# Attention of a two-layer diffusion trunk: the probabilities of wide head pairs are divided by their sums before they are turned

## The reference, cut to what matters

```
def one_block(q_blk):
    s = jnp.einsum('bqkgd,btkd->bkgqt', q_blk, k, preferred_element_type=jnp.float32) * scale
    p = jax.nn.softmax(s, axis=-1).astype(v.dtype)
    return jnp.einsum('bkgqt,btkd->bqkgd', p, v)
```

## Time and profile before

| | us |
|---|---|
| time, median of 3 runs | 3545.4 (3539.25, 3545.4, 3545.46) |
| the profiled execution: its time | 3544.38 |
| the profiled execution: its span, first to last instruction | 3542.6 |
| TensorE matmuls busy | 3365.2 (95% of the span) |
| VectorE busy | 1865.5 (53%) |
| ScalarE busy | 1164.7 (33%) |
| GpSimd busy | 421.8 (12%) |
| mean granted clock of TensorE | 0.983 of full speed |

### The profile page before, as it was taken

The page is one execution under the profiler, slowest core; times in us unless marked ns, Lnnn a source line. Parts: engine busy times, 40 slices in busy tenths (PEclk is TensorE's granted clock), DMA queues, the critical chain, the costliest instruction groups (busy, mean ns, idle before and its releaser), DMA issues. The chain is left out here.

```text
span 3542.6 us, 69052 instructions
## 1 busy us (share of the span) xinstructions
PE 3365.2 (95%) x28748; PEld 2885.1 (81%) x28748; DVE 1865.5 (53%) x2801; ACT 1164.7 (33%) x1778; POOL 421.8 (12%) x286
## 2 busy tenths in 40 slices
PE   6999999999888899999999999999999978889999
PEld 5888888885668878888888888888885668779897
DVE  4552554665765555543544552554644755555353
ACT  3321222226652233322222331222226533244231
POOL 2000002004313211000001000002004333120000
PEclk9999999999999999999999999999999999999999
DMA  5222221440000012222221221221430000022222
GB/s 196 98 95 67 94 92 61 144 155 30 2 17 3 3 54 78 94 96 67 100 86 58 100 100 65 96 92 53 147 112 30 2 18 3 15 83 91 93 89 95
DMA packets 68262, 263.49 MB, mean 74 GB/s; under 512 B 7536, under 2 KB 8688, under 8 KB 67440
## 3 DMA queue, kind: packets, MB, share of 16 engines
q1 hardware_dynamic: 67648, 256.95, 21.2%
q10 hardware_dynamic: 432, 3.88, 0.3%
HBM read 258.70 MB, written 2.10 MB: 74 GB/s over the span
## 5 line engine op out<-in xcount | busy, mean ns | idle before, releaser
L240 PE MATMUL ps<-hn_hi,w_hi 128*128 128x512 f32 (+1 forms) x3520 | 872.4, 329 | 16.1 <-DVE hn_lo L447 5.9
L240 PE MATMUL ps<-hn_hi,w_lo 128*128 128x512 f32 (+1 forms) x3520 | 873.4, 329 | 0.0
L240 PE MATMUL ps<-hn_lo,w_hi 128*128 128x512 f32 (+1 forms) x3520 | 868.8, 328 | 0.0
L217 ACT ACTIVATE w_hi<-raw 128x1024 fp32r<-128x1024 f32 (+1 forms) x300 | 338.6, 1129 | 1380.3 <-PE ps L240 1222.7
L222 DVE TENSOR_TENSOR w_lo<-raw,w_hi 128x1024 fp32r<-128x1024 f32 (+1 forms) x300 | 396.7, 1322 | 481.5 <-ACT w_hi L217 473.6
L240 PEld LDWEIGHTS ps<-hn_hi,w_hi 128*128 128x128 f32 x3520 | 547.5, 190 | 83.4 <-issue 17.7
L240 PEld LDWEIGHTS ps<-hn_lo,w_hi 128*128 128x128 f32 x3520 | 547.9, 190 | 61.3
L240 PEld LDWEIGHTS ps<-hn_hi,w_lo 128*128 128x128 f32 x3520 | 544.2, 190 | 61.1
L240 PE MATMUL ps<-g_hi,w_hi 128*128 128x512 f32 (+1 forms) x1424 | 398.3, 347 | 6.8 <-DVE g_lo L881 6.8
L240 PE MATMUL ps<-g_lo,w_hi 128*128 128x512 f32 (+1 forms) x1424 | 404.0, 351 | 0.0
L240 PE MATMUL ps<-g_hi,w_lo 128*128 128x512 f32 (+1 forms) x1424 | 398.6, 347 | 0.0
(11 more groups left out here) (272 smaller groups left out, 4241.2 us busy)
## 6 DMA issues: line engine op xcount, KB each, us to landing
raw<-wgu SPq DMA_DIRECT2D x176, 512.0 KB, 3.6
w_mod_one<-wmod SPq DMA_DIRECT2D x109, 512.0 KB, 3.5
raw<-wdn SPq DMA_DIRECT2D x64, 704.0 KB, 4.0
raw<-win SPq DMA_DIRECT2D x44, 512.0 KB, 4.7
w_mod_two<-wmod SPq DMA_DIRECT2D x19, 512.0 KB, 5.6
raw<-wout SPq DMA_DIRECT2D x16, 512.0 KB, 3.5
w_mod_first<-wmod_first SPq DMA_DIRECT2D x2, 2048.0 KB, 19.0
w_mod_first<-wmod_first SPq DMA_DIRECT2D x1, 4096.0 KB, 30.4
```

What stands on the lines that cost most here:

```text
L217: act.activation(w_hi[s][:, 0:kt, :].rearrange("p k n -> p (k n)"), raw[s][:, 0:kt * P], ACT.Copy).then_inc(hi_ready[s].sem, 1)
L240: mm = pe.matmul(out[:, o:o + b - a], w[:, k, :], m[:, k, a:b], start=(k == 0 and w is w_hi[s] and m is mov_hi), stop=(k == kt - 1 and w i ...
```

## The change

For wide pairs (`normed(n)`), the division moves from the end to the front. As soon as both sums of pair n are there, VectorE takes the reciprocals at the end of its own turn n (not in turn n+1), and then multiplies head 0's 128 x 768 probabilities by them in place (`norm_first`); ScalarE does the same to head 1's at the end of its turn n (`norm_second`). TensorE's turn of a head waits for these products instead of for the exponentials. In exchange `weigh` has no spreading products, ScalarE no `copy_sums`, and `weighed` is a plain copy from PSUM, which waits for `weigh` itself. Narrow pairs are as before.

```
--- before.py
+++ after.py
@@ -1316,6 +1316,8 @@
         SHIFTED = U_NQ - U_RW
         MIX_TILE = {"mla": 0, "na": 4, "gqa": 6}
 
+        probs_normed = [sem(f"probs_normed{i}") for i in range(2)]
+
         def attention(l, nt):
             pairs = [(m, qt, hp) for m in ("mla", "na", "gqa") for qt in range(nt // P) for hp in range(2)]
             N = len(pairs)
@@ -1376,6 +1378,11 @@
                 return pairs[n][0] == "mla"
             act_scaled = [2 * sum(scaled_by_act(j) for j in range(n)) for n in range(N + 1)]
             buf = lambda n, i: 2 * (n % 2) + i
+
+            def normed(n):
+                return not one_bank(n)
+            normed_until = [sum(normed(j) for j in range(n)) for n in range(N + 1)]
+            spread_until = [n - normed_until[n] for n in range(N + 1)]
 
             with nc.Block() as block:
                 @block.tensor
@@ -1396,7 +1403,10 @@
                                 mm.then_inc(scores_ready[i].sem, 1)
 
                     def turn(n, i):
-                        pe.wait_ge(exp_ready[i].sem, exp_ready[i].at(n + 1))
+                        if normed(n):
+                            pe.wait_ge(probs_normed[i].sem, probs_normed[i].at(normed_until[n + 1]))
+                        else:
+                            pe.wait_ge(exp_ready[i].sem, exp_ready[i].at(n + 1))
                         for c, kts in enumerate(key_tiles(n)):
                             if 2 * n + i >= 1:
                                 pe.wait_ge(probs_t_ready[c].sem, probs_t_ready[c].at(2 * n + i))
@@ -1413,9 +1423,12 @@
                         kts = [kt for c in key_tiles(n) for kt in c]
                         for kt in kts:
                             for i in range(2):
-                                pe.matmul(ps[half(i), 6 + n % 2, 0:P], values(n, i, kt),
-                                          probs_t[:, buf(n, i), kt * P:(kt + 1) * P], start=(kt == kts[0]),
-                                          stop=(kt == kts[-1]))
+                                mm = pe.matmul(ps[half(i), 6 + n % 2, 0:P], values(n, i, kt),
+                                               probs_t[:, buf(n, i), kt * P:(kt + 1) * P], start=(kt == kts[0]),
+                                               stop=(kt == kts[-1]))
+                        if normed(n):
+                            mm.then_inc(pv_ready.sem, 1)
+                            return
                         pe.wait_ge(sum_inverted.sem, sum_inverted.at(n + 1))
                         for i in range(2):
                             c = 8 + buf(n, i)
@@ -1454,6 +1467,12 @@
                                        scale=head_rstd[:, qt, stat:stat + 1],
                                        accum_out=stats[:, 4 + b:5 + b]).then_inc(exp_ready[i].sem, 1)
 
+                    def norm_second(n):
+                        b = buf(n, 1)
+                        act.wait_ge(sum_inverted.sem, sum_inverted.at(n + 1))
+                        act.activation(probs[:, b, :], probs[:, b, :], ACT.Copy,
+                                       scale=stats[:, 8 + b:9 + b]).then_inc(probs_normed[1].sem, 1)
+
                     def copy_first(n, i):
                         act.wait_ge(probs_turned[0].sem, probs_turned[0].at(2 * n + i + 1))
                         if n >= 2:
@@ -1475,12 +1494,14 @@
                         late_sums = n < N and not one_bank(n)
                         if late_sums:
                             exps(n, 1)
-                        if n >= 2:
+                        if n >= 2 and not normed(n - 2):
                             copy_sums(n - 2)
                         if n < N and not late_sums:
                             exps(n, 1)
                         if 1 <= n <= N:
                             copy_first(n - 1, 1)
+                        if n < N and normed(n):
+                            norm_second(n)
 
                 @block.gpsimd
                 def _(pool):
@@ -1548,9 +1569,20 @@
                         b = buf(n, 0)
                         dve.reciprocal(stats[:, 8 + b:10 + b], stats[:, 4 + b:6 + b]).then_inc(sum_inverted.sem, 1)
 
+                    def norm_first(n):
+                        b = buf(n, 0)
+                        dve.wait_ge(sum_inverted.sem, sum_inverted.at(n + 1))
+                        dve.tensor_scalar(probs[:, b, :], probs[:, b, :], stats[:, 8 + b:9 + b], None,
+                                          ALU.mult).then_inc(probs_normed[0].sem, 1)
+
                     def weighed(n):
                         m, qt, hp = pairs[n]
-                        dve.wait_ge(sums_spread.sem, sums_spread.at(n + 1))
+                        if normed(n):
+                            dve.wait_ge(pv_ready.sem, pv_ready.at(n + 1))
+                            dve.tensor_copy(mix[:, MIX_TILE[m] + hp, qt * P:(qt + 1) * P],
+                                            ps[:, 6 + n % 2, 0:P]).then_inc(mix_ready.sem, 1)
+                            return
+                        dve.wait_ge(sums_spread.sem, sums_spread.at(spread_until[n + 1]))
                         o, r = ps[:, 6 + n % 2, 0:P], sums_inv[:, n % 2, :]
                         dst = mix[:, MIX_TILE[m] + hp, qt * P:(qt + 1) * P]
                         if m == "na" and latent(n):
@@ -1568,15 +1600,19 @@
                         if 1 <= n <= N:
                             if not between:
                                 copy_second(n - 1, 0)
-                            invert_sums(n - 1)
+                            if not normed(n - 1):
+                                invert_sums(n - 1)
                         if n >= 2:
                             weighed(n - 2)
                         if 1 <= n <= N:
                             copy_second(n - 1, 1)
+                        if n < N and normed(n):
+                            invert_sums(n)
+                            norm_first(n)
             for x, n in ((scores_ready[0], N), (scores_ready[1], N), (biased, biases[N]), (raw_max, 2 * N - act_scaled[N]), (max_scaled, act_scaled[N]), (max_ready[0], N), (max_ready[1], N),
                          (exp_ready[0], N), (exp_ready[1], N), (probs_turned[0], 2 * N), (probs_turned[1], 2 * N),
                          (probs_t_ready[0], 2 * N), (probs_t_ready[1], 2 * N), (pv_ready, N), (sum_inverted, N),
-                         (sums_spread, N), (mix_ready, N), (keep_ready, 2), (shift_step, 4 * SHIFTED)):
+                         (sums_spread, spread_until[N]), (probs_normed[0], normed_until[N]), (probs_normed[1], normed_until[N]), (mix_ready, N), (keep_ready, 2), (shift_step, 4 * SHIFTED)):
                 x.phase_end(n)
 
 
```

24 lines of the change are left out of this document (21 added, 3 removed).

## The result

The changed kernel takes 3552.54 us (median of 21 runs, 3547.5 to 3556.2); the kernel before took 3545.11 on the same chips (21 runs, 3538.9 to 3550.83). The ratio is 1.0021, with an interval of 1.0015 to 1.0027: slower by 7.4 us, which is just over the 0.2% that can be told here. The profiled execution took 3556.2 us and is the slowest of the 21, while that of the kernel before (3544.38) lies just under its median: the two profiles differ by more than the medians do.

A forecast was written before the change was run, and what follows sets the result against it. The prediction took the loop of scores, maxima, exponentials and next scores to bound `mla` and `gqa`. Its terms, -0.4 + 1.8 + 0.8 + 0 = +2.2 us, gave a forecast of 3547.5 us, range 3541 to 3555.

The forecast's parts named there:

- the picture of the steady pairs: Attention: `gqa` pairs stay at 5.05 us, `mla` pairs take 5.74 to 6.6, with the new products hidden but for small slips.
- The ring: `mla` and `gqa`: scores, maxima, exponentials of both heads, next scores set the pair's time; nothing the change removes is in it.
- TensorE as the real limit of `mla`: Rival, chance 0.07: each of 10 `mla` pairs gives back all of 0.32 us, for a time of 3542.
- T + 6.3: `mla`, T being the start of a pair's scores: VectorE's product starts near here, leaving 0.48 us before the next maximum.
- U + 5.55: `gqa`, U being the start of a pair's scores: reciprocal ends here, VectorE's product at U + 6.12; cost 0.
- Their prices: The added 128 x 768 products: 0.56 us on VectorE and 0.84 on ScalarE, from the nearest rows, at cost 0.
- GpSimd catches the product, +1.8: `mla`: GpSimd's long operations delay VectorE's product, mean slip 0.18 us a pair over 10 pairs; bounds 0 to +8.4.
- the prediction's two terms: `mla`, 10 steady pairs: +1.8 us for slips behind GpSimd, -0.4 for the spreading products removed from TensorE.
- VectorE holds GpSimd up too, more of `na` beside it, +0.8: `na`, both layers: GpSimd's shifts end later, so about 2.1 us more of `na` runs beside them; 0 to 1.3.
- Edges 0, give or take 1.5: Last wide pairs of `mla` and `gqa`, both layers: exposed products and removed work sum to 0 us.
- The rival on the clock: Rival, chance 0.04: in `gqa` TensorE gives up busy time and the clock falls, +19 us, for 3566.
- My last sign of being wrong: Changed profile: the prediction is wrong if low-clock stretches appear that were not there.

The follow-up runs named there:

- c2: The changed kernel run again with no edit, as a control: 3553.32 us, ratio 1.0019.
- e2: The changed kernel with only the wide pairs of `mla` divided first, `gqa` as before the change: 3554.99 us (6 runs), ratio 1.0031.
- r2: The changed kernel with the input projection's next weight block loaded ahead of the modulation load that waits for VectorE: 3550.03 us, ratio 1.0015.
- c1: The kernel before run again with no edit, as a control: 3545.67 us, ratio 0.9999.
- n1: The kernel before with two more semaphores created and never used: 3545.93 us, ratio 0.9999.
- r1: The kernel before with the input projection's next weight block loaded ahead of the modulation load that waits for VectorE: 3543.44 us, ratio 0.9998.
- n3: The kernel before with 100 one-column fills of a spent buffer on GpSimd per layer, behind its token shifts: 3544.1 us, ratio 0.9998.
- e5: The kernel before without GpSimd's token shifts, which are left out of the computation: 3538.78 us, ratio 0.9987.
- e3: The changed kernel without GpSimd's token shifts, which are left out of the computation: 3545.36 us, ratio 1.0002.
- p2: The changed kernel with TensorE's two spreading products of a wide pair put back, into columns nobody reads: 3547.49 us (12 runs), ratio 1.0009.
- e1: The changed kernel with only the wide pairs of `gqa` divided first, `mla` as before the change: 3548.49 us, ratio 1.0013.
- e4: The changed kernel with both heads' products on ScalarE, none on VectorE: 3551.97 us, ratio 1.0018.

## Why the prediction was right or wrong

The time fell into the range, and the picture of the steady pairs was right. That the range held is partly luck, since it was made wide for caught products and most of the loss came from elsewhere; the measured +7.4 is over three times the +2.2 of the sum. What failed is the claim behind the sum that the change costs only what it does on the path inside attention. No term stood for the clock at the edge or for stages outside. Point by point:

- *The ring is unchanged; `gqa` pairs stay at 5.05.* Right: 985.23 - 980.18 = 5.05, with the same 0.18. TensorE as the real limit of `mla` is out: the pairs take 5.79, not 5.5.
- *Where the products stand.* Placed at T + 6.3 in `mla`: it was T + 6.44. Placed at U + 5.55 in `gqa`: 985.75 - 980.18 = U + 5.57.
- *Their prices.* 0.56 on VectorE measured 0.62, and 0.84 on ScalarE measured 0.94: each a tenth too small, and hidden as foreseen. The estimate of 0.46 from the Trainium skill (VectorE: DVE Perf Modes, TRN2 errata) was further off than the row.
- *GpSimd catches the product, +1.8.* Caught they were: 784 ns in the mean over the first layer's 16 pairs, up to 1.37 us there and 1.56 in the second. In the first profile the slip hardly came: one pair in either layer is 0.1 to 0.2 longer, and `mla` takes 61.23 us against 61.20 in the first layer, and 48.36 against 48.32 in the second. Other profiles of the changed kernel show it as the prediction has it. In the second layer of c2 one product takes 1.90, the next maximum starts 0.91 after it was due, and the pair takes 2744.95 - 2738.27 = 6.68:

```profile
2738.27 2.82 PE L1401 MATMUL ps<-k_mla,q_mla 96*128 96x512 f32 x8
...
2738.92 1.90 DVE L1575 TENSOR_SCALAR probs<-probs,stats 128x768 f32<-128x768 f32 x1
...
2744.95 2.39 PE L1401 MATMUL ps<-k_mla,q_mla 96*128 96x512 f32 x6 [0.45 <-ACT probs L1466]
```

  What decides is the first pair. Where it takes 13.5 us, GpSimd and the pairs meet kindly and 0.1 to 0.2 is lost; in all five cases in which it takes 12.5 or 11.2 (c2 once, e2 and r2 twice), 1.0 to 1.4 is lost in that layer's `mla`. Against an unchanged `mla` with the same first pair (61.20 and 60.23; 48.32, 47.35 and 46.04 us), both layers together lose 0.1 in the first profile, 1.0 in c2, and 2.4 in e2 and in r2. The mean, 1.5, is what the prediction's two terms come to (+1.8 and -0.4). So this part was right in kind and size.
- *VectorE holds GpSimd up too, more of `na` beside it, +0.8.* Right in kind. GpSimd's 128 x 768 operation went from 1466 to 1516 ns, so it is held as well; here this case's trace agrees with the Trainium skill (SBUF — State Buffer, Who interferes with whom), which the earlier trace rows could show for one side only. GpSimd is busy 7.41 us in `na` in place of 5.34. Its price came by another way than the one I summed: one 128 x 1 product held for 1.46, at the moment when TensorE depends on it.
- *Edges 0, give or take 1.5.* At the edge from `mla` to `na` of the first layer this is the term that was mis-sized: `na` took 2.7 more (44.38 to 47.07), since the clock fell. In the second layer, -0.5 (37.37 to 36.88), and there a clock event went away: `na` has a granted clock of 0.95 in the kernel before (0.91 to 0.95 in four of its profiles and its kin, before, c1, n1, r1; 1.00 in n3 and e5), and 1.00 in all eight profiles with the change.
- *The rival on the clock* was right that the clock can fall, but had the wrong place and cause. I looked for it in `gqa`, where TensorE gives up busy time, and priced it at 19 us. It came behind a wait of TensorE for VectorE's held product, not where busy time was given up. It struck in the 8 us behind the `mla` pairs and cost 2 to 3. My last sign of being wrong, low-clock stretches that were not there, did show; but the second profile of the kernel before has this one too, so it is an event that comes without the change too and that the change made more frequent here. It is in all four profiles that have the change in `mla` with a product on VectorE, GpSimd's shifts beside it and TensorE's products gone (after, c2, e2, r2: `na` 46.8 to 47.4), and in one of the five of the kernel before and its inert or reordered kin (c1).
- *The whole.* Predicted +2.2 in all, measured +7.4 by the medians. Attention gave +1.3 and +0.3 in the two pairs of profiles, of which the second started the second layer's `mla` with 1.0 us less of low clock in the changed kernel. By the medians, 1 to 2 of this are weights that land late in the input projection (r2 against r1), 1 or 2 go with GpSimd (e3 against e5), neither clear of zero; and about 5, which may overlap with these, come back when TensorE's two products are put back (p2).

**What stays open.** The cause of most of the 7.4 us. p2 shows that the program without the two products is slower than the one with them. It doesn't show whether their work or their place in the program does it. For `na` the traces speak against the work: what sorts the profiles is how long VectorE's small product is held beside GpSimd, that is, where GpSimd's operation stands when `na` begins, and p2 moved that as well. For the input projection they offer nothing: it ends over 40 us ahead of the first changed instruction, yet it takes 191.4 to 193.9 in the six profiles of kernels with TensorE's full instruction count (before, c1, n1, n3, e5, p2) and 194.5 to 197.6 in the six of kernels with fewer (after, c2, e1, e2, e3, e4), all with the old order of the loads. Whether that is the length of TensorE's program, or where its code lies, was not told apart. The start is unexplained as well, and it doesn't go with the change: the first product stands at 50.1 to 50.4 us in five of the seven profiles that lack TensorE's products and in p2, but at 48.8 and 47.9 in e3 and e4, and at 50.6 in e5, which has no change. The granted clock from 25 to 50 us is 0.70 in the changed kernel and 0.76 in the kernel before.

## What to carry to other kernels

Taking work off an engine that isn't what a stage waits for gained nothing here, and the whole became slower. A change also shifts the engines against each other: ask at each edge behind it which small operations will now meet a helper engine's long one, and whether TensorE's wait for them, here 1.56 us in place of 0.72, is followed by a stretch at the lower clock. An operation that can be held by a helper engine is a risk where it stands ahead of what the next stage waits for, at edges (one product of 128 x 1) and in the steady loop (a slack of 0.48 us was used up in some executions and not in others). Where a change of a few us is judged, take several profiles of both kernels and cut them by stage, and look first at the stages that were not touched.

## What was not expected of the hardware

- The same 512 KB weight load of an unchanged stage took 4.65 us from issue to use in one profiled execution and 5.87 in the other.
- Two products for each of 32 pairs, whose results nobody reads, made a kernel faster by 5 us of 3550.
- A product over 128 x 1 on VectorE (0.16 us beside an idle GpSimd) took 1.46 when it was issued 0.02 us after an operation of GpSimd of 1.47 began, and 1.03 when issued 0.45 after it.
- Low clock comes in stretches of some 3 to 14 us at the lower of the two levels. Summed over the span, length times (1 - granted clock), the kernel before has 59 us, of which 5 lie in the first attention stage, and 62 in its repeat; with the change it is 63, of which 8.5 in that stage, and 67. It doesn't tell the kernels apart by itself: e4 has 53 at a span of 3548.6. The spread of 9 to 12 us between executions of one kernel goes along with the clock: the 21 runs of the changed kernel average 3554.4 us at a mean clock of 0.982 (8 runs) and 3550.2 at 0.984 (5 runs).
- A pass of ScalarE from SBUF to SBUF with a scale per partition takes 0.936 us for 128 x 768, where one without such a scale took 0.844.
